# How the RMSNorms of a transformer trunk sum their squares and spread 1/rms: the last two tiles' squares go to TensorE, and W_o's last residual changes places

## What is computed

```python
def rmsnorm(x, w):
    y = x * lax.rsqrt(jnp.mean(x * x, axis=-1, keepdims=True) + EPS)
    return y * w
def modulate(h, shift, scale): return h * (1 + scale) + shift
def swiglu(h, wg, wu, wd):     return (jax.nn.silu(h @ wg) * (h @ wu)) @ wd

for i in range(2):
    a_lat = modulate(rmsnorm(x_lat, norm1_w[i]), sh1, sc1)      # norm 0; in layer 1: N3
    a_ctx = modulate(rmsnorm(x_ctx, norm1_w[i]), csh1, csc1)
    m_lat, m_ctx = mixer_i(a_lat, a_ctx)   # ssd: rmsnorm(y * silu(z), gnorm_w) @ w_out (the gated norm)
    x_lat = x_lat + g1 * m_lat             # attention: (...) @ w_o
    x_lat = x_lat + g2 * swiglu(modulate(rmsnorm(x_lat, norm2_w[i]), sh2, sc2), ...)   # N2, N4
    # the context likewise in layer 0, not needed in layer 1
return rmsnorm(x_lat, final_norm_w)                             # N5
```

## Time and profile before

| | us |
|---|---|
| median of 3 executions (lowest to highest) | 1262.17 (1261.96 to 1263.51) |
| span of the profiled execution, first to last instruction | 1261.4 |
| median above that span | 0.8 |
| TensorE matmuls busy | 1162.0 (92%) |
| VectorE busy | 887.9 (70%) |
| ScalarE busy | 609.2 (48%) |
| gated norm, from the last sum to the first W_out matmul | 409.65 to 417.66 |
| N2, N3 (parts a and b) | 493 to 531, 851 to 887 |
| N4 | 1061 to 1073 |
| N5 and output | 1250 to 1261 |

### The profile page before, as it was taken

One profiled execution on the slowest core, in us unless ns is written; L12 is line 12 of the kernel. 1 busy time (PEld: TensorE's weight loads), 2 busy tenths in 40 slices (PEclk: granted clock), 3 DMA queues, 4 the chain that ended last, 5 costly groups with the idle time before them and its releaser, 6 DMA issues.

```text
span 1261.4 us, 20628 instructions
## 1 busy us (share of the span) xinstructions
PE 1162.0 (92%) x7476; PEld 696.6 (55%) x7476; DVE 887.9 (70%) x1403; ACT 609.2 (48%) x1082; POOL 90.0 (7%) x102
## 2 busy tenths in 40 slices
PE   3999999899897899899999999997899996999997
PEld 2545444454443347544444444476555585888886
DVE  5695876958767976588787879835466767655654
ACT  4564654646557422633333332215545464566642
POOL 0004013050130000000000000000000000000000
PEclk9999999999999799999999999999999998899998
DMA  9423222221232353155555555431222114455552
GB/s 389 155 72 129 67 88 79 67 100 67 91 110 72 129 201 134 68 200 200 200 202 197 211 179 212 176 121 68 100 71 82 57 59 161 139 200 200 192 187 90
DMA packets 24536, 174.09 MB, mean 138 GB/s; under 512 B 2720, under 2 KB 2720, under 8 KB 5536
## 3 DMA queue, kind: packets, MB, share of 16 engines
q1 hardware_dynamic: 18432, 128.24, 28.0%
q0 software_dynamic: 4608, 33.56, 7.6%
q10 hardware_dynamic: 1440, 11.53, 2.6%
HBM read 172.27 MB, written 1.05 MB: 137 GB/s over the span
## 4 chain that ended last, share of the span: by engine, by line
PE 76%; DVE 12%; ACT 6%; issue 4%; DMA 1%; DVEq 0%; ACTq 0%; POOL 0%; SPq 0%; POOLq 0%
PE bank L1659 21%; PE bank L1661 20%; PE bank L1660 20%; DVE wl L937 2%; ACT wh L425 2%; PE bank L1834 2%; DVE arena L1119 1%; PE bank L2079 1%; PE bank L2093 1%; ACT arena L467 1%; PE bank L1863 1%; DVE arena L1180 1%; PE bank L1680 1%; PE bank L1848 1%; PE bank L1844 1%
## 5 line engine op out<-in xcount | busy, mean ns | idle before, releaser
L1659 PE MATMUL bank<-hh,wh 128*128 128x512 f16 (+1 forms) x1168 | 394.7, 338 | 18.7 <-ACT arena L527 5.9
L1661 PE MATMUL bank<-hh,wl 128*128 128x512 f16 (+1 forms) x1168 | 394.1, 337 | 0.0
L1660 PE MATMUL bank<-hl,wh 128*128 128x512 f16 (+1 forms) x1168 | 394.0, 337 | 0.0
L937 DVE SCALAR_TENSOR_TENSOR wl<-raw,wh 128x1024 f16<-128x1024 f32 x224 | 267.5, 1209 | 172.2 <-ACT wh L425 170.1
L425 ACT ACTIVATE wh<-raw 128x1024 f16<-128x1024 f32 x224 | 229.2, 1042 | 253.3 <-PE bank L1661 204.0
L1659 PE MATMUL bank<-arena,wh 128*128 128x256 f16 (+1 forms) x620 | 194.5, 314 | 6.8 <-DVE arena L1407 2.8
L1660 PE MATMUL bank<-arena,wh 128*128 128x256 f16 (+1 forms) x620 | 194.4, 314 | 0.0
L1661 PE MATMUL bank<-arena,wl 128*128 128x256 f16 (+1 forms) x620 | 194.3, 313 | 0.0
L1659 PEld LDWEIGHTS bank<-hh,wh 128*128 128x128 f16 x1168 | 115.2, 99 | 119.6 <-issue 34.2
L1661 PEld LDWEIGHTS bank<-hh,wl 128*128 128x128 f16 x1168 | 115.0, 98 | 87.9 <-issue 0.6
L1660 PEld LDWEIGHTS bank<-hl,wh 128*128 128x128 f16 x1168 | 115.0, 98 | 77.6 <-issue 5.9
(11 more groups left out here) (248 smaller groups left out, 1341.4 us busy)
## 6 DMA issues: line engine op xcount, KB each, us to landing
raw<-wgu SPq DMA_DIRECT2D x44, 1024.0 KB, 4.8
arena<-wadaT POOLq DMA_DIRECT2D x32, 1024.0 KB, 5.0
raw<-wdn SPq DMA_DIRECT2D x16, 896.0 KB, 4.6
...
arena<-wada SPq DMA_DIRECT2D x8, 1024.0 KB, 19.2
...
```

The lines of the kernel that those rows point to most:

```text
L937: ve.scalar_tensor_tensor(wl[:, u.slot, a:b], raw[:, u.slot, a:b], WS, wh[:, u.slot, a:b], ALU.mult, ALU.subtract).then_inc(lo_done, 1)
L1659: pe.matmul(o, wh[:, u.slot, wsl], ahi[:, k, a:e], start=st, stop=False)
L1660: pe.matmul(o, wh[:, u.slot, wsl], alo[:, k, a:e], start=False, stop=False)
L1661: i = pe.matmul(o, wl[:, u.slot, wsl], ahi[:, k, a:e], start=False, stop=en)
```

## The change

Four edits, in all norms:

1. The last pair of squares is no longer added by VectorE. `total` on TensorE runs `ssum` over `ssq` (which lacks that pair) and then, in `last_pair`, over each of the two `sq` tiles, accumulating in the same bank. `root` waits for the last.
2. `rdg` is gone. `bcast` takes the column of 1/rms itself, repeated 128 times, as weights and the identity as the moving side, one float32 matmul of 128 columns for each 128 tokens.
3. The hooks move. N2a and N3a: sums behind k 2 and broadcast behind k 5 of the same pass. N2b and N3b: sums behind k 5 of the first unit's context pass, broadcast behind k 1 of the second's. In the gated norm, the two `wl` halves of unit U_OUT+1 are made inside the tile loop (at k=2 and k=8), no longer around `inverse`; in `halves` of VectorE `cvt_half(u0, 0)` stands ahead of `inverse`.
4. The W_o loop is written out. Its last turn converts only the second half of U_GU1, then does residual m=3; `columns` moves ahead of it. N4 then uses `h_part`, with both halves of U_GU1+1 converted in between; `h_lo` and `h_hi` are gone. N4 and N5 broadcast into bank 4 (`YB`).

```diff
@@ scalar
-            def root(n, width, cs, ce=4):
+            def root(width, squares, cs, ce=4):
-                act.wait_ge(c_ss, n + 1)
+                act.wait_ge(ssd, squares)
@@ scalar, W_o
-            with act.Fori(0, 2) as i:
-                for m in range(2):
-                    cvt_on(Unit(U_WO + m + 1, 2, i))
-                    square_pair(i * 4 + (SQ_X[4] + 2 * m), i * 4 + 2 * m, TC, i * 4 + (XU[4] + 2 * m))
-            cvt_half(Unit(U_GU1 + 1), 1, UF // 2, UF)
-            root(N4, D, 2)
-            h_hi(N4, TC)
+            for m in range(3):
+                cvt_on(Unit(U_WO + m + 1))
+                square_pair(SQ_X[4] + 2 * m, 2 * m, TC, XU[4] + 2 * m)
+            cvt_half(Unit(U_GU1), 1, UF // 2, UF)
+            square_pair(SQ_X[4] + 6, 6, TC, XU[4] + 6)
+            root(D, SQ_X[4] + 8, 2)
+            u1 = Unit(U_GU1 + 1)
+            h_part(N4, 1, {1: (u1, 0, 0, UF // 2), 5: (u1, 1, UF // 2, UF)})
@@ vector, halves (N2, N3)
                 residual(6, GB[2:4], 0, TC)
-                sums(squares, 0, TC)
+                cvt_half(u0, 0, 0, UF // 2)
                 inverse(ns[0], 0, 2)
-                cvt_half(u0, 0, 0, UF // 2)
...
                 cvt_half(u1, 1, UF // 2, UF)
-                sums(squares + 2, TC)
                 inverse(ns[1], 2)
@@ vector, W_o
+            for m in range(4):
+                if m < 3:
+                    cvt_on(Unit(U_WO + m + 1))
+                else:
+                    columns(1, cc("n2w", KC, 2 * KC), 24)
+                    cvt_half(Unit(U_GU1), 1, UF // 2, UF)
+                ve.wait_ge(unit_done, 2 * (U_WO + m) + UD + 2)
+                residual(2 * m, GB[2 * (m % 2):2 * (m % 2) + 2], TC)
+                if m < 3:
+                    sums(SQ_X[4] + 2 * m, TC)
             inverse(N4, 2)
-            h_lo(N4, TC)
+            h_part(N4, 1, {1: (u1, 0, 0, UF // 2), 5: (u1, 1, UF // 2, UF)})
@@ tensor
+            def last_pair(squares, cs, ce=4):
+                for m in range(2):
+                    pe.wait_ge(sqd, squares + m + 1)
+                    ssum(sq[:, m, :], cs, ce, stop=(m == 1)).then_inc(ssd, 1)
+            def total(squares, cs, ce=4):
+                pe.wait_ge(ssd, squares)
+                ssum(ssq, cs, ce, start=True)
+                last_pair(squares, cs, ce)
             def bcast(n, cs, ce=4, bank=OB[1]):
-                pe.wait_ge(c_dg, n + 1)
-                pe.matmul(bank[:, cs * P:ce * P], ones, rdg[:, cs * P:ce * P], start=True, stop=True).then_inc(c_bc, 1)
+                pe.wait_ge(c_rr, n + 1)
+                for c in range(cs, ce):
+                    i = pe.matmul(bank[:, c * P:(c + 1) * P], rt[:, c:c + 1].to_broadcast([P, P]), ident, start=(c == cs), stop=True,
+                                  skip_group_check=True)
+                i.then_inc(c_bc, 1)
@@ tensor, N2 (N3 alike)
-                     hooks=({5: lambda: half_sum(N2[0], SQ_X[2] + 6, 0)}, {0: lambda: half_bcast(N2[0], 0)})[hf])
+                     hooks={2: lambda: half_sum(SQ_X[2] + 6, 0), 5: lambda: half_bcast(N2[0], 0)} if hf == 0 else None)
-                                 hooks={4: lambda: half_sum(N2[1], SQ_X[2] + 6, 1), 7: lambda: half_bcast(N2[1], 1)} if (h, s) == (0, 1) else None)
+                                 hooks={(0, 0): {5: lambda: half_sum(SQ_X[2] + 6, 1)}, (0, 1): {1: lambda: half_bcast(N2[1], 1)}}.get((h, s)))
```

More of the change, by code:

```diff
@@ L478, in halves @@
                 cvt_half(u0, 0, 0, UF // 2)
-                root(ns[0], D, 0, 2)
+                root(D, squares + 2, 0, 2)
                 h_part(ns[0], 0, {1: (u0, 1, UF // 2, UF), 5: (u1, 0, 0, UF // 2)})
@@ L482, in halves @@
                 square_pair(squares + 2, k0, TC, up + 2)
-                root(ns[1], D, 2)
+                root(D, squares + 4, 2)
                 h_part(ns[1], 1, {})
-            def h_hi(n, t0):
-                for k in range(KC):
-                    act.wait_ge(n32_ok, HN[n] * KC + k + 1)
-                    act.activation(hh[:, k, t0:T], n32[:, k % 2, t0:T], ACT.Copy).then_inc(hh_ok, 1)
             def evac_pre(u, g, tile, b):
@@ L655, in ada0_out @@
                     act.activation(apart4[:, j, :], GB[2 + j % 2][:, 0:UN], ACT.Copy).then_inc(a0_out, 1)
-            root(0, D, 0)
+            act.wait_ge(c_ss, 1)
+            root(D, KC, 0)
             act.wait_ge(in_kp, 16)
@@ L741, in _ @@
             last_group(NG - 1, Unit(U_TAIL))
-            root(1, DI, 0)
+            root(DI, SQ_G + 16, 0)
             act.dma_start(x[:, :, :], xT).then_inc(in_x_again, 16)
@@ L1432, in ffn @@
                     residual(2 * m, GB[2 * (m % 2):2 * (m % 2) + 2], t0)
-                    sums(SQ_X[3 + 2 * layer] + 2 * m, t0)
+                    if m < 3:
+                        sums(SQ_X[3 + 2 * layer] + 2 * m, t0)
             ve.wait_ge(ada_ok, ADA_OUT)
@@ L1557, in _ @@
             o_lo(3)
-            with ve.Fori(0, 2) as i:
-                for m in range(2):
-                    cvt_on(Unit(U_WO + m + 1, 2, i))
-                    ve.wait_ge(unit_done, i * 4 + (2 * (U_WO + m) + UD + 2))
-                    residual(i * 4 + 2 * m, GB[2 * m:2 * m + 2], TC)
-                    sums(i * 4 + (SQ_X[4] + 2 * m), TC)
-            cvt_half(Unit(U_GU1 + 1), 1, UF // 2, UF)
-            columns(1, cc("n2w", KC, 2 * KC), 24)
+            for m in range(4):
[6 more added lines that the diff above has]
+                residual(2 * m, GB[2 * (m % 2):2 * (m % 2) + 2], TC)
+                if m < 3:
+                    sums(SQ_X[4] + 2 * m, TC)
             inverse(N4, 2)
-            h_lo(N4, TC)
+            u1 = Unit(U_GU1 + 1)
+            h_part(N4, 1, {1: (u1, 0, 0, UF // 2), 5: (u1, 1, UF // 2, UF)})
             ffn(1, U_GU1, U_DN1, TC, False)
@@ L1669, in _, with ssum @@
             H = (hh, hl)
[L1671 removed]
+            def ssum(tile, cs, ce=4, start=False, stop=False):
                 for c in range(cs, ce):
[L1674 to L1680 removed]
+                    i = pe.matmul(OB[0][:, c:c + 1], tile[:, c * P:(c + 1) * P], ones[:, 0:1], start=(start and c == cs), stop=stop,
+                                  skip_group_check=True)
+                return i
+            def last_pair(squares, cs, ce=4):
[6 more added lines that the diff above has]
+                last_pair(squares, cs, ce)
+            def bcast(n, cs, ce=4, bank=OB[1]):
+                pe.wait_ge(c_rr, n + 1)
+                for c in range(cs, ce):
+                    i = pe.matmul(bank[:, c * P:(c + 1) * P], rt[:, c:c + 1].to_broadcast([P, P]), ident, start=(c == cs), stop=True,
+                                  skip_group_check=True)
+                i.then_inc(c_bc, 1)
             def ada_part(g, b):
@@ L1729, in _ @@
             pe.wait_ge(ssd, KC)
-            ssum(0, 0)
+            ssum(ssq, 0, start=True, stop=True).then_inc(c_ss, 1)
             pe.wait_ge(s2_ok, 2)
@@ L1950, in _ @@
                     pe.matmul(OB[0][:, c:c + 1], part[:, j, :], ones[:, 0:1], start=(c == 2 and j == 0), stop=False, skip_group_check=True)
-            pe.wait_ge(ssd, SQ_G + 16)
-            for c in (2, 3, 0, 1):
-                i = pe.matmul(OB[0][:, c:c + 1], ssq[:, c * P:(c + 1) * P], ones[:, 0:1], start=False, stop=True, skip_group_check=True)
-            i.then_inc(c_ss, 1)
+            pe.wait_ge(ssd, SQ_G + 14)
+            ssum(ssq, 0)
+            last_pair(SQ_G + 14, 0)
             bcast(1, 0)
@@ L2008, in ffn, with norm @@
                              ready=(al_ok, 2 + n0 + a) if m == 0 else None)
-            def norm(n, cs, sums):
-                pe.wait_ge(ssd, sums)
-                ssum(n, cs)
-                bcast(n, cs)
+            def norm(n, squares, bank):
+                total(squares, 2)
+                bcast(n, 2, 4, bank)
             ffn(0, U_GU0, U_DN0, 0, HN[N2[0]] * KC)
@@ L2165, in _ @@
                 wo_mm(m, range(KC))
-            norm(N4, 2, SQ_X[5])
+            norm(N4, SQ_X[4] + 6, YB)
             ffn(1, U_GU1, U_DN1, TC, HN[N4] * KC)
-            norm(N5, 2, SQ_X[5] + KC)
+            norm(N5, SQ_X[5] + 6, YB)
 def packed(w, units):
```

52 lines of the change are left out of this document (13 added, 39 removed).

## The result

The kernel before took 1263.23 us (median of 19 executions, 1261.17 to 1264.82), the changed kernel 1265.18 us (19 executions, 1264.43 to 1265.88). The ratio is 1.0016, with a 95% interval of 1.0010 to 1.0022: the change costs 1.3 to 2.8 us. It is slower, by less than the 0.2% at which the prediction draws its line, though the interval reaches just over it. The forecast was 1264.8 us and +2.55 us. That the time itself came within 0.4 us of 1264.8 is partly luck: this time the kernel before stood 1.06 us above the 1262.17 from which the sum was made, so the difference to be compared with +2.55 is +1.95.

The account below looks back on a forecast made before the run. TensorE, busy 1162.0 of 1261.4 us, bounds the kernel; time changes only where it waits or clocks low. Gated 0, N2 +0.55, N3 +2.2, N4 +1.1, N5 -1.3 give +2.55: span 1263.95, plus 0.8, 1264.8 us; range 1258.5 to 1267.0.

Parts of the forecast that it names:

- the sum: All places: gated 0, N2 +0.55, N3 +2.2, N4 +1.1, N5 -1.3 give +2.55 us.
- part a: First half of N2 and N3: root held behind a delayed conversion, first tile later by 0.6 and 1.3 us.
- part b: Second half of N2 and N3: clock falls over TensorE's gaps; N2b starts +0.55 us, N3b +2.2 us.
- N4: After W_o: first tile 4.1 us earlier, slower tiles, lower clock may last longer; +1.1 us.
- N5: Last norm: sum ends 0.63 us earlier and no `rdg` product; -1.3 us.
- Rival B: N2 and N3: part a not late, root held by the sums alone; 1262.9 us; chance 15%.
- The other half of the argument: N2 and N3: at full clock part b would start 19.15 us behind part a's start.
- Rival A: N2b and N3b: clock holds over the gaps, moved hooks pay; -3.7 us, 1258.5 us; chance 15%.
- Gated norm: Gated norm: first tile 0.5 us earlier, against two conversions inside the loop; 0, from -0.8 to +0.6 us.
- Norm 0: First norm: no change, since other TensorE matmuls cover the `rdg` product.
- The chances: Whole kernel, against a 0.2% (2.5 us) line: slower 0.48, the same 0.38, faster 0.14.
- The fall of the clock: N2b and N3b: TensorE's gaps before the sums lower its clock at both norms; 0.95 plus 1.7 us.

Follow-up runs that it names:

- i3: The changed kernel with root and reciprocal put ahead of the u0 conversion in part a of N2 and N3; 1262.00 us, ratio 0.9997.
- i4: The changed kernel with the second half of U_GU1+1 converted behind N4's eight tiles, not at tile 5; 1262.82 us, ratio 1.0001.
- h1: The changed kernel with unread 256-column matmuls filling TensorE's waits in part b of N2 and N3; 1259.29 us, ratio 0.9974.
- (3): The changed kernel with N2b's and N3b's sums behind k 0 and broadcast behind k 2 of the second unit's context pass; 1258.28 us, ratio 0.9969.

## Why the prediction came out as it did

Most mechanisms held; the sizes at part a, part b, N4 and N5 were off, and partly cancel. At N4 the mechanism itself was right only in part.

- **Part a**: forecast +0.6 and +1.3, measured +0.44 and +1.10. Rival B is refuted, the root stood behind the conversion. The conversion was moved back by 1.25 us and not by 12 x 0.125 = 1.5 (it starts 3.86 us behind the residual, before 2.61). Successive sums overlap: the first, of 0.50 us, starts at 494.08, and the next two, of 1.03 together, at 494.45; the product's next matmul starts at 495.34, 1.26 us behind the start of the first sum.
- **Part b**: forecast 21.8 us from part a to part b, measured 22.37 and 22.34. The term that was too small is the low stretch behind the sums, taken as long as in the kernel before (3.4 us, worth 1.7). It was 5.0 us at N2 (516.2 to 521.2), 6.9 with the sums, and longer at N3, so that all four k passes behind the sums ran at 1.27 us: 2.5 us, near the upper bound of 2.8 that I had kept. That makes part b 0.55 later at each norm. The other half of the argument held to 0.1 us: with the clock kept up it was 19.09, forecast 19.15. Rival A is refuted: the twelve one-column passes did not keep the clock, nor did 52 more.
- **N4**: forecast +1.1, measured +0.57, on average over the traces with the same edit +0.5. The tiles took the 13.9 us forecast. The first tile came 4.8 us sooner and not 4.1 (it starts 12.37 us behind the residual of m=1, before 17.21), so the last `hl` came 0.2 us sooner than before and not 0.55 later. The forecast had the first low stretch last on through tiles 5 to 7. It ended at 1077.6, and a second one began at 1080.9, behind the wait for tile 5: these tiles did run at the lower clock, for another reason, and what comes behind the last `hl` takes 0.75 us more than in the kernel before. N4's code alone does not settle whether it falls, since in two of six traces with the same N4 it did not.
- **N5**: forecast -1.3, measured -1.51. In the other traces it is -1.0 to -1.5, by whether the broadcast runs at the full clock (0.71 us in the changed kernel) or at the lower one (1.22 in i3 and i4).
- **Gated norm**: forecast 0, measured +0.11: from the root to the first tile 0.7 us less (forecast 0.5), from there to the residual ahead of N2 0.8 more. **Norm 0**: forecast 0, and its own steps took the same.
- **The sum**: forecast +2.55, the places of the change give +2.73. Of the trace's difference of 1.7 us, -0.99 is the load of x landing earlier. The ten other traces have the first tile of norm 0 at 19.1 to 19.7 us, and the one trace of the kernel before at 20.19; whether that is chance or comes with the change is open, and the measured +1.95 lies between the two readings.
- **The chances**: most weight, 0.48, stood on "slower by over 0.2%", and it is 0.16% (0.10 to 0.22); a result within 0.2% had 0.38. The forecast lay just above that line (2.55 against 2.5 us) and the result 0.04% below it, so the chances say little for or against the reasoning; what is missing is no larger than the start's microsecond.
- **The fall of the clock** at part b, which I had taken from the rows although only one of two gaps of 2.5 us had brought it: it came at both norms, and its price is 3.3 us at each (h1). Single gaps of 2.44 and 2.45 us were enough at six of seven places.

What I did not see is that there is a better place than either. I followed the change's hooks and compared them with the old ones. The change's sums stand ahead of their operand, where TensorE waits for it, and its broadcast stands four passes behind the sums, though 1/rms is ready 0.5 us behind them. Both hooks later than the change's and sooner than the old ones (3) are worth 5.9 us. A broadcast put sooner with the sums left where the change has them was not tried.
